# Opening transfers reordered, up projections in two PSUM banks, and value loads issued by ScalarE in a two-layer hybrid decoder step

## The reference

```
h = rmsnorm(x)
p = h @ w_in                     # all q, k, v, gates: 5916 columns
a = nsa(q, k, v)                 # compressed + selected + window attention, 8 heads
b = stick_breaking(q, k, v)      # 4 heads: w = exp(logsig(z) + sum of later logsig(-z))
c = fox(q, k, v, logf)           # 4 heads: softmax with cumulated forget values
u = g0*(a @ w_up_nsa) + g1*(b @ w_up_sb) + g2*(c @ w_up_fox)
x = x + u @ w_out
x = x + (silu(h2 @ w_gate) * (h2 @ w_up)) @ w_down      # h2 = rmsnorm(x)
```

## Time and profile before

| | us |
|---|---|
| median of three runs | 2769.57 |
| the three runs | 2766.76, 2772.31, 2769.57 |
| profiled execution | 2762.04 |
| its span, first to last instruction | 2760.0 |
| PE busy | 2512.1 (91%) |
| DVE busy | 936.0 (34%) |
| POOL busy | 653.3 (24%) |
| ACT busy | 527.3 (19%) |
| mean granted clock of PE | 0.951 |

### The profile page before, as it was taken

The page is one execution under the profiler, slowest core; times in us unless marked ns, Lnnn a source line. Parts: engine busy times, 40 slices in busy tenths (PEclk is TensorE's granted clock), DMA queues, the critical chain, the costliest instruction groups (busy, mean ns, idle before and its releaser), DMA issues.

```text
span 2760.0 us, 43519 instructions
## 1 busy us (share of the span) xinstructions
PE 2512.1 (91%) x13426; PEld 1948.8 (71%) x13426; DVE 936.0 (34%) x1905; ACT 527.3 (19%) x1336; POOL 653.3 (24%) x588
## 2 busy tenths in 40 slices
PE   4999788887999999999999988888789999999997
PEld 3887544444688888888888864445457888888886
DVE  3114555321241442333231155552112244223423
ACT  1013222213222111110000232222232221111100
POOL 0000122120142333443300001212112242444331
PEclk9999999788999999999999989997889999999998
DMA  6244344154121222222424334432612221222121
GB/s 199 69 130 116 101 131 132 35 163 145 63 92 62 92 78 75 92 73 68 155 75 133 96 107 120 125 104 79 176 56 92 92 92 62 92 92 83 47 93 39
DMA packets 288298, 270.90 MB, mean 98 GB/s; under 512 B 50882, under 2 KB 249746, under 8 KB 287810
## 3 DMA queue, kind: packets, MB, share of 16 engines
q1 hardware_dynamic: 271266, 258.43, 30.7%
q10 hardware_dynamic: 16800, 9.61, 1.2%
HBM read 258.36 MB, written 17.97 MB: 100 GB/s over the span
## 4 chain that ended last, share of the span: by engine, by line
PE 80%; DVE 7%; SPq 5%; issue 5%; ACT 1%; POOL 0%; DMA 0%; DVEq 0%; POOLq 0%; ACTq 0%
PE ps L1110 33%; PE ps L1236 9%; PE ps L637 6%; PE ps L712 5%; PE ps L713 5%; SPq L612 3%; PE ps L1006 3%; PE ps L778 2%; PE ps L931 2%; PE ps L822 2%; PE ps L870 2%; PE ps L671 1%; PE ps L670 1%; PE ps L719 1%; DVE arena L1780 1%
## 5 line engine op out<-in xcount | busy, mean ns | idle before, releaser
L1110 PE MATMUL ps<-hT,ring 128*128 128x260 f32 x1344 | 306.4, 385 | 5.6 <-DVE hT L1708 5.6
L1110 PEld LDWEIGHTS ps<-hT,ring 128*128 128x128 f32 x1344 | 257.1, 191 | 46.3 <-DVE hT L1708 6.4
L1594 POOL TENSOR_SCALAR ring<-ring,rr,gnat 128x31 f32<-128x31 f32 (+2 forms) x192 | 100.7, 534 | 519.5 <-DVE rr L1826 273.1
L1110 PE MATMUL ps<-hT,units 128*128 128x260 f32 x928 | 213.2, 382 | 0.0
L1110 PEld LDWEIGHTS ps<-hT,units 128*128 128x128 f32 x928 | 176.3, 190 | 27.1
L712 PE MATMUL ps<-hT,ring 128*128 128x260 f32 x640 | 193.1, 383 | 0.0
L713 PE MATMUL ps<-hT,ring 128*128 128x260 f32 x640 | 192.8, 383 | 0.0
L637 PE MATMUL ps<-cst,ring 128*128 128x128 f32 (+1 forms) x704 | 130.3, 298 | 56.1 <-ACT ring L1434 20.6
L637 PEld LDWEIGHTS ps<-cst,ring 128*128 128x128 f32 (+1 forms) x704 | 79.8, 145 | 114.9 <-issue 57.2
L1110 PE MATMUL ps<-arena,units 128*128 128x260 f32 x704 | 158.1, 383 | 0.4 <-DVE arena L2070 0.4
L1110 PEld LDWEIGHTS ps<-arena,units 128*128 128x128 f32 x704 | 133.6, 190 | 21.6 <-issue 1.2
(11 more groups left out here) (325 smaller groups left out, 4422.1 us busy)
## 6 DMA issues: line engine op xcount, KB each, us to landing
ring<-in_w_in SPq DMA_DIRECT2D x20, 2048.0 KB, 8.2
units<-in_cache_fox_kv SPq DMA_DIRECT2D x192, 128.0 KB, 2.2
units<-in_cache_sb_kv SPq DMA_DIRECT2D x192, 128.0 KB, 2.2
ring<-in_w_ffn_gate SPq DMA_DIRECT2D x22, 1024.0 KB, 5.4
ring<-in_w_ffn_up SPq DMA_DIRECT2D x22, 1024.0 KB, 8.0
ring<-in_w_ffn_down SPq DMA_DIRECT2D x16, 1408.0 KB, 6.2
units<-in_cache_nsa_cmp_kv SPq DMA_DIRECT2D x96, 128.0 KB, 2.7
units<-in_cache_nsa_sel_kv SPq DMA_DIRECT2D x192, 64.0 KB, 1.9
```

The source lines that it names most:

```text
L1110: last = mm(ps[:, bank, 0:H2], w[:, k, :], a[:, k, :], start=first and k == 0, stop=True, skip_group_check=True)
L1594: last = nc.gpsimd.tensor_scalar(p, p, one, gnat[:, i, c:c + 1], ALU.mult, ALU.mult)
```

## The change

Four things are edited.

1. The opening. The identity, x_prompt and x_sample come first, with a semaphore x_in of their own, and PE starts on these three. The rest of cst, the page table and the loop follow on SP; SP waits for the page table only ahead of the first unit. The gains (as 40 rows of 128), cmp_pos, the masks and b_forget are issued by ACT. PE transposes the gains behind x and cmp_pos, and DVE copies them. The first chunk of w_in is one transfer: the array in memory has its first 512 columns in the order that the kernel wants. The copy of s_win stands behind chunk 3.
2. The up projections. From the eighth on, every second one uses bank 2, and PE waits for the copy before the last one. The second sb tile of `merge` waits for the last copy.
3. The sbv units of the sequences 1 to 7 are issued by ACT, at the places of `value_s` in PLAN; each time it loads four page numbers into registers, waits for the slot and issues four transfers. SP issues the other units.
4. The number of unit slots, eight with six of their own, is the same in both files.

```diff
+UP_BANK = [2 if n >= 7 and n % 2 else 7 for n in range(len(UPS))]
...
+        scales = ar(5120 + DEPTH * P, P)[0:(2 * DEPTH + 1) * KD]
...
-            dma(cst[:, :], A["consts"][:, 0:NKEEP]).then_inc(sems["const_in"], 16)
-            dma(hT[...][:, 0:NCONST - NKEEP], A["consts"][:, NKEEP:NCONST]).then_inc(sems["const_in"], 16)
-            dma(xnat[:, 0:TT], A["x_prompt"][0]...).then_inc(sems["const_in"], 16)
-            dma(xnat[0:NS, TT], A["x_sample"]...).then_inc(sems["const_in"], 16)
-                for i in range(DEPTH):
-                    dma(gam[:, 2 * i, :], A["norm_mix_g"][i].rearrange("(k p) -> p k", p=P)).then_inc(sems["const_in"], 16)
...
+            dma(ident, A["consts"][:, 0:P]).then_inc(sems["x_in"], 16)
+            dma(xnat[:, 0:TT], A["x_prompt"][0]...).then_inc(sems["x_in"], 16)
+            dma(xnat[0:NS, TT], A["x_sample"]...).then_inc(sems["x_in"], 16)
+            dma(cst[:, P:NKEEP], A["consts"][:, P:NKEEP]).then_inc(sems["const_in"], 16)
             dma(pgt[:, :], A["page_table"]...).then_inc(sems["pg_in"], 16)
-            sp.wait_ge(sems["pg_in"], 16)
...
                 if ch == ("in", 0):
-                    for g in range(G):
-                        for t in range(4):
-                            dst = slot.rearrange("p (k t g d) -> p k t g d", k=KD, g=G, d=DH)[:, :, t, g, :]
-                            dma(dst, w_in[:, :, g * 256 + t * DH:g * 256 + (t + 1) * DH]).then_inc(sem, 16)
+                    put(0, KD, 512, w_in[:, :, 0:512])
...
-                dma(out["s_win"]..., A["state_nsa_win_kv"]...).then_inc(sems["win_dma"], 16)
                 for n in range(RING + 3):
                     load_chunk(l, n)
+                    if n == RING:
+                        dma(out["s_win"]..., A["state_nsa_win_kv"]...).then_inc(sems["win_dma"], 16)
+                sp.wait_ge(sems["pg_in"], 16)
...
                 for n in range(OWN_SLOTS, NU):
-                    load_unit(l, n)
+                    if UNITS[n][0] != "sbv" or UNITS[n][1] == 0:
+                        load_unit(l, n)
...
-            pe.wait_ge(sems["const_in"], 16 * 11)
+            pe.wait_ge(sems["x_in"], 16 * 3)
...
+            pe.wait_ge(sems["const_in"], 16 * 9)
             for i in range(DEPTH):
-                last = tp(ps[:, 4, i * STRIDE:(i + 1) * STRIDE], posn[:, i, :], STRIDE)
-            last.then_inc(sems["post_ps"], 1)
+                tp(ps[:, 4, i * STRIDE:(i + 1) * STRIDE], posn[:, i, :], STRIDE)
+            tp(ps[:, 4, DEPTH * STRIDE:...], scales, (2 * DEPTH + 1) * KD).then_inc(sems["post_ps"], 1)
...
-                    pe.wait_ge(sems["up_ev"], at(pe, "up_ev", l, n))
+                    pe.wait_ge(sems["up_ev"], at(pe, "up_ev", l, n if n < 7 else n - 1))
...
-                            elif m == 3:
+                            elif m in (1, 3):
                                 wait("up_ev", 16)
...
+            dma = act.dma_start
+            for j, g in enumerate([... five gain vectors ...]):
+                dma(scales[j * KD:(j + 1) * KD], g.rearrange("(k p) -> k p", p=P)).then_inc(sems["const_in"], 16)
+            dma(posn[:, :, :], A["cmp_pos"]...).then_inc(sems["const_in"], 16)
+            dma(hT[...][:, 0:NCONST - NKEEP], A["consts"][:, NKEEP:NCONST]).then_inc(sems["const_in"], 16)
+            dma(bfb[:, :, :], A["b_forget"]...).then_inc(sems["const_in"], 16)
             act.wait_ge(sems["const_ok"], 1)
+            act.wait_ge(sems["pg_in"], 16)
...
+            def value_s(l, b, h):
+                last = 2 * b + h - 1
+                if last < 0 or last // 2 == NS - 1:
+                    return
+                b, h = last // 2, last % 2
+                n = UNITS.index(("sbv", b + 1, h))
+                slot, sem = unit_slot(n), sems[f"u{n % USLOTS}"]
+                for i in range(4):
+                    act.reg_load(pages[i], pgt[0:1, (b + 1) * NPG + 4 * h + i:(b + 1) * NPG + 4 * h + i + 1])
+                name, read = unit_read[n - USLOTS]
+                act.wait_ge(sems[name], at(act, name, l, read))
+                rows = A["cache_sb_kv"].rearrange("l n r t h d -> (l n) r (t h d)")
+                for i in range(4):
+                    pg = act.snap(pages[i], min_val=0, max_val=NPOOL - 1)
+                    act.dma_start(slot[:, i * 256:(i + 1) * 256], rows[dl[0] * NPOOL + pg][:, 256:512]).then_inc(sem, 16)
...
-            dve.wait_ge(sems["const_in"], 16 * 11)
-            v.memset(epsb[:, :], EPS)
-            v.tensor_copy(identb, ident)
-            last = v.tensor_copy(maskb[:, P:4 * P], hT[...][:, 0:3 * P])
-            last.then_inc(sems["const_ok"], 1)
+            v.memset(epsb[:, :], EPS).then_inc(sems["const_ok"], 1)
...
-                v.tensor_copy(UP[:, 4 * br + c, h * H2:(h + 1) * H2], ps[:, 7, 0:H2]).then_inc(sems["up_ev"], 1)
+                v.tensor_copy(UP[:, 4 * br + c, h * H2:(h + 1) * H2], ps[:, UP_BANK[n], 0:H2]).then_inc(sems["up_ev"], 1)
...
+            dve.wait_ge(sems["post_ps"], 1)
+            v.tensor_copy(posT[:, :, :], ps[:, 4, 0:DEPTH * STRIDE]...)
+            v.tensor_copy(gam[:, :, :]..., ps[:, 4, DEPTH * STRIDE:...])
+            v.tensor_copy(identb, ident)
+            v.tensor_copy(maskb[:, P:4 * P], hT[...][:, 0:3 * P]).then_inc(sems["init_z"], 1)
+            dve.wait_ge(sems["init_z"], 2)
             norm(0, 0, lambda k: gam[:, 0, k:k + 1])
```

More of the change, by code:

```diff
@@ L204, in w_dmas @@
 def w_dmas(ch):
-    return {"cmp": 2, "up": 4, "ffn": 2}.get(ch[0], {("in", 0): 8, ("in", 2): 2}.get(ch, 1))
+    return {"cmp": 2, "up": 4, "ffn": 2}.get(ch[0], {("in", 2): 2}.get(ch, 1))
 def u_dmas(u):
@@ L377, in build @@
         sems = {}
-        for name in list(PER) + ["const_in", "const_ok", "xt_ps", "xt_in", "y_ps", "y_ev", "y_dma", "win_dma", "pg_in",
+        for name in list(PER) + ["x_in", "const_in", "const_ok", "xt_ps", "xt_in", "y_ps", "y_ev", "y_dma", "win_dma", "pg_in",
                                  "post_ps", "dve_chain", "act_chain", "init_z"] \
@@ L482, in _ @@
             dma = sp.dma_start
-            dma(cst[:, :], A["consts"][:, 0:NKEEP]).then_inc(sems["const_in"], 16)
[L484 to L487, removed]
-                for i in range(DEPTH):
-                    dma(gam[:, 2 * i, :], A["norm_mix_g"][i].rearrange("(k p) -> p k", p=P)).then_inc(sems["const_in"], 16)
[L490 to L493, removed]
+            dma(ident, A["consts"][:, 0:P]).then_inc(sems["x_in"], 16)
+            dma(xnat[:, 0:TT], A["x_prompt"][0].rearrange("(t p) d -> p t d", p=P)).then_inc(sems["x_in"], 16)
+            dma(xnat[0:NS, TT], A["x_sample"].rearrange("b s d -> (b s) d")).then_inc(sems["x_in"], 16)
+            dma(cst[:, P:NKEEP], A["consts"][:, P:NKEEP]).then_inc(sems["const_in"], 16)
             dma(pgt[:, :], A["page_table"].rearrange("(a b) n -> a (b n)", a=1)).then_inc(sems["pg_in"], 16)
-            sp.wait_ge(sems["pg_in"], 16)
             def load_chunk(l, n):
@@ L615, in _ @@
                 in_layers(sp, l)
-                dma(out["s_win"].rearrange("l b r t h d -> (l b) r (t h d)")[bass.ds(l * NS, NS), 0:WIN - 1],
-                    A["state_nsa_win_kv"].rearrange("l b r t h d -> (l b) r (t h d)")[bass.ds(l * NS, NS), 1:WIN]).then_inc(sems["win_dma"], 16)
                 for n in range(RING + 3):
                     load_chunk(l, n)
+                    if n == RING:
+                        dma(out["s_win"].rearrange("l b r t h d -> (l b) r (t h d)")[bass.ds(l * NS, NS), 0:WIN - 1],
+                            A["state_nsa_win_kv"].rearrange("l b r t h d -> (l b) r (t h d)")[bass.ds(l * NS, NS), 1:WIN]).then_inc(sems["win_dma"], 16)
+                sp.wait_ge(sems["pg_in"], 16)
                 for n in range(OWN_SLOTS):
@@ L927, in up @@
                 else:
-                    pe.wait_ge(sems["up_ev"], at(pe, "up_ev", l, n))
+                    pe.wait_ge(sems["up_ev"], at(pe, "up_ev", l, n if n < 7 else n - 1))
                 k0 = (0, 4, 6)[br]
                 for k, t in enumerate(OT[br]):
-                    last = mm(ps[:, 7, 0:H2], w[:, (k0 + k) * 512 + c * P:(k0 + k) * 512 + (c + 1) * P], PT[:, t, h * H2:(h + 1) * H2],
+                    last = mm(ps[:, UP_BANK[n], 0:H2], w[:, (k0 + k) * 512 + c * P:(k0 + k) * 512 + (c + 1) * P], PT[:, t, h * H2:(h + 1) * H2],
                               start=k == 0, stop=k == len(OT[br]) - 1)
@@ L1295, in _ @@
             fn = nc.scalar.activation
+            dma = act.dma_start
+            for j, g in enumerate([A[n][i] for i in range(DEPTH) for n in ("norm_mix_g", "norm_ffn_g")] + [A["norm_final_g"]]):
+                dma(scales[j * KD:(j + 1) * KD], g.rearrange("(k p) -> k p", p=P)).then_inc(sems["const_in"], 16)
+            dma(posn[:, :, :], A["cmp_pos"].rearrange("l (m a) d -> m l (a d)", a=2)).then_inc(sems["const_in"], 16)
+            dma(hT[:, :, :].rearrange("p a b -> p (a b)")[:, 0:NCONST - NKEEP], A["consts"][:, NKEEP:NCONST]).then_inc(sems["const_in"], 16)
```

(19 more changed lines are left out.)

2 lines of the change are left out of this document (1 added, 1 removed).

## The result

The changed kernel takes 2722.94 us (median of 4, 2715.68 to 2732.09) against 2768.16 us (median of 4, 2765.7 to 2772.31): a ratio of 0.9831, 95% interval 0.9807 to 0.9855. That is 45 us less, where 54 were forecast; the forecast was 2715 us, 2692 to 2744. Its profiled execution took 2717.87 us, with a span of 2715.6 us.

What follows compares the result with a forecast made beforehand. TensorE held 80% of the chain, with SP's issue of transfers bounding the opening and the sample values. Gains of 23.4 + 6.8 + 24 = 54 us from the median 2769.57 gave 2715 us, range 2692 to 2744.

Steps and rivals of the forecast that it cites:

- Step 1, opening: Start of the kernel: first projection product at 26.0 us instead of 49.4, a gain of 23.4 us.
- Case D: Opening: weights come late, at 223 GB/s, 4 us less gain, 2719 us; shares chance 0.63 with the forecast.
- Step 2, up projections: Up projections: seven gaps of 0.48 us vanish with two banks, 3.4 us per layer, 6.8 us in all.
- Step 3, values: Sample group's values: ACT issues units, 16 us per layer gained, 12 after the tail, 24 us in all.
- 14.7 - 5: Values, per layer: full clock saves 14.7 us of busy time, less 5 us for the clock new waits keep low.
- The 7 us of new waits: Values, per layer: PE waits caused by ACT's issue, 1.5, 1.0 and 3.0 us and several under 0.5.
- The count of units: Values: of ACT's 14 units per layer, eight among the FoX blocks and six in the stick-breaking part.
- the lower bound: Values, per layer: 28 - 27 - 4 = 3 us lost if all eight units among the FoX blocks lie on the path.
- B: Values: ACT's issue is the new bound, 20 us lost per layer, slower at 2780 us; chance 0.04.
- Tail: Last value step: the last unit, issued behind head 1's last exponential, comes 2.8 us late; 4 us lost per layer with clock.
- A: Values: transfers, not SP's orders, are the limit, or ACT's units come equally late; gain 0, 2747 us; chance 0.17.
- C: Values: ACT's holds vanish under other work and the clock stays 1.00; 25 us per layer, 2689 us; chance 0.16.

Runs made afterwards that it cites:

- e3: Changed kernel with only ScalarE's wait for the page table moved behind its squares of the opening; 2720.77 us (0.9831).
- e1: Changed kernel with all sixteen up projections in bank 7 again, with the waits for their copies as before; 2734.59 us (0.985).
- e10: e3 with two value units, sbv(1,1) and sbv(4,0), issued earlier on ACT, ahead of copies where it waits for PE; 2700.69 us (0.9755).
- e2: Changed kernel with all sbv value units issued by SP again and none by ACT; 2738.81 us (0.986).
- e7: Kernel before with half the bytes in each sbv transfer and the same number of transfers; 2767.87 us (one run).
- e6: Changed kernel with ACT's page loads written twice; the repeats came out as one, so it equals the changed kernel; 2719.46 us (0.9799).
- e8: Changed kernel with the first w_in chunk again as eight transfers with rows of 256 bytes; 2723.97 us (one run).
- e9: e3 with ACT's eight opening transfers held until x is there and the page table issued ahead of x; 2731.6 us (one run).
- e5: Changed kernel with two ACT unit issues per layer put behind the exponentials and ACT's page-table wait behind the squares; 2715.32 us (0.9798).

## Why the prediction was right, and where its terms were off

The time lies in the range and the mechanism of all three parts was found, but the sizes were off both ways. The opening gave 4.0 us less than forecast and the values with the tail 8.6 less, the up products and what follows them 8.3 more, and 5.5 us were lost where nothing had been expected. That the sum came out 9 us short, and not 18, is luck. Of the signs named, two failed narrowly: the first product came at 30.03 us, where later than 30 was to count as wrong, and the clock in the values of layer 1 was 0.84, where above 0.85 was expected (layer 2: 0.86). A third did not come at all, the wait of some 3 us at the last value step.

**Step 1, opening: right in kind, 4 us too large.** Forecast 26.0 us, measured 30.03. The arrival of x is 1.8 us of it (10.42 for 8.6 us). The rates of the changed kernel in the slices of the earlier trace rows:

```profile
GB/s 0 101 330 390 413 446 319 409 338 310 410 397 385 386 386 392 376 380 157 5 0 0 0 0 0 0 0 11 0 0 0 0 0 0 0 0 0 0 0 0
```

The second and third slice carry 101 and 330 GB/s, where 175 and 405 were reckoned, and most of ACT's 0.24 MB and the first of the constants go with x. Its last packet ends at 9.57 us in the trace, for 7.8. The 0.8 us until the semaphore were right: PE starts 0.85 us later. The page table is 2.5: without ACT's wait e3 starts at 27.50 us. I had put that wait at "up to 0.5 us", reckoning only from about 12.5 us; the table landed at 14.9 us, and ACT's own table load of 1.28 us stands behind it. Of the 19.4 us another 1.1 are lost at once, since the first sixteen product instructions take 6.49 us for 5.38. Case D did not come: the weights landed at 20.04 us, where 18 were forecast and 30 feared.

**Step 2, up projections: right in kind, too small.** 3.4 us per layer forecast, 5.7 and 6.0 measured (the upper bound was 3.85). Missing from the term was the 0.25 us by which a product that waits is itself longer (e1); the gap itself is 0.51 us, not 0.48. The further 1.7 us per layer behind the up products come with the two banks too: e1 does not have them.

**Step 3, values: the mis-sized term is the clock.** The windows part the stretch into PE's busy and idle time, with the same 504 instructions. The kernel before, layer 1:

```profile
551.31:639.43 88.12, 69.90 (x504) 40.65 (x506) 17.23 (x41) 13.90 (x42) 17.12 (x16) 0.79 0.56 165
```

Before, this layer was 69.90 busy and 18.2 idle; after, 67.10 and 12.7; in e10 63.62 and 8.1. So the waits fell by 5.5 us, and 13.1 - 7 = 6.1 were forecast; but busy time fell by 2.8 us where 14.7 - 5 = 9.7 were forecast. The means over all profiles say the same, with 4.5 us less idle and 1.3 less busy. With SP as issuer (six stretches: before, e2, e7) the values are 87.4 us, 69.4 busy and 18.0 idle; with ACT in the changed kernel's order (fourteen: the changed kernel twice, e1, e3, e6, e8, e9) they are 81.6, 68.1 busy and 13.5 idle. The idle time hardly varies, 17.1 to 19.1 and 12.7 to 14.2 us; the busy time does, 67.1 to 71.4 and 64.2 to 74.4 us, with the clock. The gain is 5.7 us per layer where step 3 had 16 ahead of the tail. e10, without the two waits, has 15.7.

The 7 us of new waits were right as a sum (6.4 for exponentials and 1.2 for units were measured), but by luck, since the list was wrong: I had let the scores go ahead without the exponential before them, and so had waits of 1.5, 1.0 and 3.0 and several small ones. In fact two of 3.2 us reach PE whole, and behind the one shown PE stood at half clock for some 10 us. The count of units was wrong too: not eight but ten of the fourteen stand among the FoX blocks and not six but four in the stick-breaking part, so that the lower bound would have been 28 - 34 - 4 = -10 us per layer, and the argument against B was weaker than it looked.

**Tail:** the loss of 4 us per layer did not come; the last value step comes 39.58 and 40.00 us behind the stick-breaking product, against 39.75 and 41.37. The last unit's orders were reckoned from the end of head 1's exponential. In the trace they begin 0.22 us behind its start: ACT's queue issues while the engine still computes (ACT, then PE's last value step).

```profile
646.80 1.24 ACT L1475 ACTIVATE ring<-ps 128x1280 f32<-128x1280 f32 x1
647.02 1.90 ACTq L1427 DMA_DIRECT2D ring<-in_cache_sb_kv  x4
```

```profile
650.69 0.40 PE L1069 MATMUL ps<-units,arena 128*32 128x256 f32 x1 [0.24 <-DMA ring<-in_cache_sb_kv]
```

PE waits 0.24 us where 2.8 were forecast.

**Rivals.** A falls by e2 and e7. The Trainium skill, "DMA: Bandwidth & Descriptors", section "Issuing engines are not separate DMA queues", calls the sequencer's time usually small; this trace does not agree, with 11.3 us of waits left at half the bytes (e7) and 1.2 when a second engine issues. B's mechanism exists, ACT's issue ahead of exponentials, but at 6.4 us of PE's time per layer, far from the 43 at which it decides. C did not come; e10 reaches 15.7 of C's 25 us per layer, at a clock of 0.88 and not 1.00.

**What was given back.** The stretch ahead of the values has no edit in it but the opening's, and still it grew: before and e7 501.9 to 507.7 us, mean 504.6; the eleven kernels with the new opening 499.5 to 511.6, mean 507.6. Layer 2, the kernel before and then the changed one:

```profile
1391.70:1896.01 504.31, 452.06 (x2857) 318.65 (x2857) 205.30 (x509) 112.07 (x340) 56.03 (x108) 0.94 0.35 100
```

```profile
1357.41:1865.80 508.39, 457.25 (x2856) 320.97 (x2857) 205.38 (x509) 112.40 (x340) 56.30 (x108) 0.92 0.36 108
```

The same instructions are 5.2 us longer busy at a lower clock. Some 6 us over both layers go this way on the mean. Why the clock falls at other places is not settled: e5 has 499.53 and e10 504.30 us in layer 2. The copy of s_win, which moved in both layers, was not tested by itself.

## What to carry to other kernels

If a queue's orders are the chain, another engine can issue a part of them, but each order is then an instruction of that engine: put it where that engine waits for someone else, ahead of a step whose result is wanted late, and not ahead of the one that the bound engine wants next. Count a wait of the bound engine twice, as idle time and as the slower clock behind it: two waits of 3.2 us per layer were worth 9.8 us, 5.4 of them idle time. And look at what a wait is queued ahead of: ScalarE needed the page table only 500 us later, and waiting for it at the start cost 2.5 us.

## What the runs showed that was not expected

A few words can be long under way: the page table, ordered at 2.56 us among the opening's transfers, landed 12.3 us after its issue; the 128 KB units took 2.2 us.

The same idle time is not always followed by the same clock. In layer 1, some 189 us behind the last up product, PE waits 3.13 us in both kernels; the sixteen instructions behind it take 5.42 us in the kernel before and 3.77 in the changed one, at a granted clock of 0.51 and 1.00 (926.5 to 930.0 and 893.8 to 897.3 us):

```profile
926.56 5.42 PE L1110 MATMUL ps<-PT,ring 128*128 128x260 f32 x16 [3.13 <-DVE PT L2022]
```

```profile
893.84 3.77 PE L1105 MATMUL ps<-PT,ring 128*128 128x260 f32 x16 [3.13 <-DVE PT L2038]
```

These 1.65 us are the gain in the table's last line (1.58 in layer 1); all kernels with two banks take 3.77 us here in both layers, and those with one bank (before, e7, e1) 5.3 to 5.5. Why is open. And one program's times go with its mean clock: the changed kernel took 2715.68 us at 0.960, 2717.87 at 0.957, 2728.01 at 0.951 and 2732.09 at 0.950.
